# Gate and up products of both feed-forward layers: seven block products in place of eight

## What is computed

```python
def swiglu(x, w_gate, w_up, w_down):
    return (jax.nn.silu(x @ w_gate) * (x @ w_up)) @ w_down

x = layer_norm(ALPHA * x + mix.astype(x.dtype), ln_mix_g[i], ln_mix_b[i])
x = layer_norm(ALPHA * x + swiglu(x, w_ffn_gate[i], w_ffn_up[i], w_ffn_down[i]), ln_ffn_g[i], ln_ffn_b[i])
gate = jax.nn.sigmoid(x @ w_ple_gate[i] + b_ple_gate[i])
```

## Time and profile before

| | us |
|---|---|
| median of three executions | 2624.71 (2622.63 to 2624.74) |
| span of the profiled execution, first to last instruction | 2621.1 |
| median less that span | 3.6 |
| PE busy | 2516.9 (96%) |
| DVE busy | 1464.8 (56%) |
| ACT busy | 1131.0 (43%) |
| POOL busy | 149.3 (6%) |

### The profile page before, as it was taken

The page is one execution under the profiler, slowest core; times in us unless marked ns, Lnnn a source line. Parts: engine busy times, 40 slices in busy tenths (PEclk is TensorE's granted clock), DMA queues, the critical chain, the costliest instruction groups (busy, mean ns, idle before and its releaser), DMA issues.

```text
span 2621.1 us, 29230 instructions
## 1 busy us (share of the span) xinstructions
PE 2516.9 (96%) x12112; PEld 1961.0 (75%) x12112; DVE 1464.8 (56%) x1543; ACT 1131.0 (43%) x1285; POOL 149.3 (6%) x165
## 2 busy tenths in 40 slices
PE   7998996999999999999999999999989999999998
PEld 4677883888888886877757768888768667888876
DVE  3685545888888886545675343333363744323344
ACT  3423223787777776322354242222252734222223
POOL 1001011110101100000000100000100010000010
PEclk9898997999999999999999999999999999999999
DMA  7123213999999996322202222232312012232220
GB/s 272 56 99 133 101 47 154 345 363 370 359 361 358 361 358 251 154 86 83 90 2 79 97 73 83 94 105 73 113 65 101 29 55 82 77 109 97 74 95 33
DMA packets 64565, 388.74 MB, mean 148 GB/s; under 512 B 13360, under 2 KB 13488, under 8 KB 22576
## 3 DMA queue, kind: packets, MB, share of 16 engines
q1 hardware_dynamic: 53712, 373.20, 38.9%
q0 software_dynamic: 9280, 8.42, 0.9%
q10 hardware_dynamic: 1440, 5.24, 0.5%
HBM read 391.00 MB, written 20.97 MB: 157 GB/s over the span
## 4 chain that ended last, share of the span: by engine, by line
PE 87%; DVE 5%; ACT 3%; DMA 3%; issue 1%; POOL 0%; SPq 0%; ACTq 0%; DVEq 0%; POOLq 0%
PE psD L2877 72%; PE psD L2885 1%; PE psA L2050 1%; DMA ring<-w_dense 1%; DMA ring<-w_moe 1%; PE psA L1097 1%; DVE ring_r L2502 1%; PE psA L2950 1%; ACT ring_r L2286 1%; PE psA L3080 1%; PE psA L1973 1%; PE psA L3140 1%; PE psD L2100 1%; PE psA L2088 1%; PE psA L2930 1%
## 5 line engine op out<-in xcount | busy, mean ns | idle before, releaser
L2877 PE MATMUL psD<-rounded,ring_r 128*128 128x512 f32 (+1 forms) x6168 | 1456.4, 397 | 15.7 <-DVE ring_r L2502 12.3
L2877 PEld LDWEIGHTS psD<-rounded,ring_r 128*128 128x128 f32 (+1 forms) x6168 | 1155.2, 188 | 315.3 <-issue 24.0
L2502 DVE TENSOR_TENSOR ring_r<-ring,ring_r 128x2048 fp32r<-128x2048 f32 (+3 forms) x143 | 307.1, 2147 | 232.5 <-ACT ring_r L2286 228.8
L2877 PE MATMUL psD<-ring_r,rounded 128*128 128x512 f32 (+1 forms) x1728 | 412.6, 395 | 5.7 <-DVE rounded L983 2.4
L2286 ACT ACTIVATE ring_r<-ring 128x2048 fp32r<-128x2048 f32 (+3 forms) x143 | 251.9, 1762 | 366.0 <-PE psD L2877 359.5
L2877 PEld LDWEIGHTS psD<-ring_r,rounded 128*128 128x128 f32 x1728 | 320.0, 191 | 86.4 <-issue 8.7
L978 DVE TENSOR_TENSOR ring_r<-ring,ring_r 128x2048 fp32r<-128x2048 f32 x128 | 293.2, 2291 | 44.4 <-ACT ring_r L776 42.3
L776 ACT ACTIVATE ring_r<-ring 128x2048 fp32r<-128x2048 f32 x128 | 245.2, 1917 | 58.0 <-DMA ring<-w_moe 33.4
L2877 PE MATMUL psD<-rounded,rounded 128*128 128x512 f32 x768 | 192.1, 399 | 0.0
L1828 DVE TENSOR_TENSOR arena<-arena,psD 128x512 f32<-128x512 f32 x44 | 30.2, 687 | 255.3 <-ACT arena L1523 255.3
L2877 PEld LDWEIGHTS psD<-rounded,rounded 128*128 128x128 f32 x768 | 139.8, 189 | 27.6 <-issue 0.2
(11 more groups left out here) (433 smaller groups left out, 2027.5 us busy)
## 6 DMA issues: line engine op xcount, KB each, us to landing
ring<-w_moe SPq DMA_DIRECT2D x192, 1024.0 KB, 7.3
ring<-w_dense SPq DMA_DIRECT2D x134, 1024.0 KB, 4.8
ring<-w_dense SPq DMA_DIRECT2D x16, 768.0 KB, 4.1
ring<-w_dense SPq DMA_DIRECT2D x16, 640.0 KB, 3.9
arena<-x_t SPq DMA_DIRECT2D x1, 2048.0 KB, 7.9
token_rows<-arena ACTq DMA_DIRECT2D x4, 512.0 KB, 2.6
arena<-pair_rows SPq DMA_DIRECT2D x4, 512.0 KB, 7.8
arena<-pair_rows ACTq DMA_DIRECT2D x4, 512.0 KB, 8.3
```

Source lines behind the costliest of these rows:

```text
L2502: dve.tensor_tensor(lo_, ring_of(u, nk, nco), hi, ALU.subtract).then_inc(sem("w_lo"), 1)
L2877: mm = pe.matmul(out, w[a], x[b], start=start and i == 0, stop=stop_ and i == 2)
```

## The change

Of the 22 gate/up units of a layer the first two stay as they are (`PLAIN_GU = 2`). For the other 20 (numbered `s`, 0 to 19 in layer 0 and 20 to 39 in layer 1, `FAST`) the product is made from 2x2 blocks: the weights are split into gate/up and first/second half of the 1024 channels, the activations into the channel halves and the token halves (256 tokens). Eight block products become seven, with sums of blocks before and after. Each block product is 4 k-tiles x 3 matmuls of 128x256, so a unit has 84 matmuls of 256 columns (before: 48 of 512).

- **Sums of activations**, once a layer: `input_sums` makes four sums of 128x1024 on DVE, after `ln_x`; ACT and DVE split them.
- **Sums of weights**, once a unit: DVE makes the first pair S13 (one instruction, 128x1024, `first_sums`), POOL the other two, S24 (`weight_sums`, two 128x512 additions, one after the other). Both pairs are split (`pair_hi` on ACT, `pair_lo` on DVE). The unit's own cut shrinks to three quarters (128x1536).
- **Sums of products**: `first_copy` (ACT), `early_sums` (two of 256), `middle_sums`, `last_sums` (512 each) on DVE; SiLU in two pieces of 256; the product of both (`hidden`) and its split.
- **Memory**: the sums lie in raw slot 2 and their parts and the unit's parts from slot 3 on, so gate/up units and the first half's down units load into two slots instead of four (`raw_plan`). The load of the first `ple_g` unit after a feed-forward goes to slot 3 and waits until the last down unit is done. `parts_of`, `ring_of` and `loaded` follow this plan.
- Semaphores are renamed, and the constants that POOL makes for the attention wait for another signal; the work there is the same.

```diff
+                def first_sums(s):
+                    ...
+                    loaded(dve, FAST[s])
+                    dve.tensor_tensor(block_pair(S13), block_pair(raw_quarters(s, 1, 2)),
+                                      raw_quarters(s, 0).unsqueeze(1).to_broadcast([P, 2, QUARTER]), ALU.add)\
+                       .then_inc(sem("w_sums"), 1)
...
+            def weight_sums(s):
+                pool.wait_ge(sem("w_sums"), 2 * s + 1)
+                if s % N_FAST > 0:
+                    pool.wait_ge(sem("pair_lo"), 2 * s)
+                step(pool.tensor_tensor(S24[:, 0:QUARTER], S13[:, 0:QUARTER], raw_quarters(s, 2), ALU.add))
+                pool.tensor_tensor(S24[:, QUARTER:2 * QUARTER], S24[:, 0:QUARTER], raw_quarters(s, 3), ALU.add)\
+                    .then_inc(sem("w_sums"), 1)
...
+                pe.wait_ge(sem("w_lo"), SPLIT_NO[FAST[s]] + 1)
+                counted(fast(ab[:, 0, :], own, A11, tokens(0, 0), True))
+                if s == run[0]:
+                    pe.wait_ge(group_freed(before[1]), GROUP_NO[before[1]] // 2 + 1)
...
+                pe.wait_ge(sem("pair_lo"), 2 * s + 1)
+                counted(fast(dc[:, 1, :], G13, 0, sums(0), True))
+                counted(fast(dc[:, 0, :], G13, 1, sums(2), True))
+                pe.wait_ge(sem("pair_lo"), 2 * s + 2)
+                counted(fast(ab[:, 1, :], G24, 0, sums(1), True))
+                pe.wait_ge(sem("first_copy"), s + 1)
+                counted(fast(ab[:, 0, :], own, A12, tokens(4, 0), False))
+                pe.wait_ge(sem("fast_moved"), 4 * s + 2)
+                counted(fast(dc[:, 0, :], own, A22, sums(3), False))
+                fast(dc[:, 1, :], G24, 1, tokens(4, 1), False).then_inc(sem("units_done"), 1)
...
+                    if slot == 2 and done:
+                        sp_.wait_ge(sem("pair_lo"), 2 * done[-1] + 2)
+                    if slot == 3 and done:
+                        sp_.wait_ge(sem("units_done"), last_unit(("down", layer_of(done[-1]), 1, 3)) + 1)
```

The calls on DVE stand in this order (`half` 0 is the first half):

```diff
+                input_sums()
+                plain_hidden(0)
+                plain_lo(0)
+                for half, run in enumerate(halves_of(layer)):
+                    if half == 0:
+                        ahead(FAST[run[0]])
+                        first_sums(run[0])
+                        pair_lo(run[0], 0)
+                        pair_lo(run[0], 1)
+                        plain_hidden(1)
+                        plain_lo(1)
+                    for s in run:
+                        if s > run[0]:
+                            last_sums(s - 1)
+                            pair_lo(s, 1)
+                            hidden(s - 1)
+                        early_sums(s)
+                        if s < run[-1]:
+                            first_sums(s + 1)
+                        ahead(FAST[s] + 1)
+                        if s > run[0]:
+                            hidden_lo(s - 1)
+                        if s < run[-1]:
+                            pair_lo(s + 1, 0)
+                        middle_sums(s)
```

341 lines of the change are left out of this document (282 added, 59 removed).

## The result

The changed kernel takes 2637.34 us (median of six executions, 2632.55 to 2644.28), the kernel before beside it 2625.16 us (2622.63 to 2630.07): a ratio of 1.0045 [1.0029, 1.0061]. The forecast was 2635 with a range of 2612 to 2660. The profiled execution of the changed kernel has a time of 2635.92 and a span of 2634.2 us, 13.1 more than the span before.

What follows compares the result with a forecast made beforehand. PE bounds the kernel before; in the changed one DVE's queue with POOL's holds sets 10.65 us a unit. Per layer +5.2 - 2.2 + 1.4 = +4.4, two layers +8.8, with semaphores +10: 2635 us, range 2612 to 2660.

Steps and rivals of the forecast that it cites:

- 1.5 us added for semaphores: Whole kernel: allowance for the second semaphore that five of DVE's ten instructions a unit wait for, priced by no row.
- Block products on PE: Gate/up units on PE: 84 matmuls of 256 columns at 0.120 us, 10.08 us a unit against 11.20.
- rival a: Steady units: PE stays the bound at 10.08 us, POOL's additions falling beside other DVE work; total -8, 2617 us; chance 0.20.
- DVE, one unit: DVE's queue in a gate/up unit: ten instructions, 9.02 us of durations, 8.44 us with overlaps, under PE's 10.08.
- POOL against DVE: Steady units: POOL additions and two-SBUF-input DVE instructions exclude each other; each addition holds DVE 1.11 us, giving 10.66 a unit.
- PE's wait in a unit: Steady units: PE waits about half a microsecond each, except the first three of each ten, at about 10.1 us.
- Start of a layer: First gate/up half: PE waits 4 us, then until 34.4, clock loses 1.7; first unit +11.2, nine others -6.0, together +5.2.
- Second half: Second ten gate/up units: PE waits 3.6 us, 1.7 for the clock, units save 7.5; together -2.2 us a layer.
- Loads: Second half's first down unit: its load and cut end late, +1.4 us a layer; first ple unit's load hidden, 0.
- Sum: Whole kernel: +4.4 us a layer, two layers +8.8, rounded up for semaphores to +10; time 2635 us.
- b: Steady units: DVE and POOL together exceed the old 11.20, units of 11.5, +16.6 us a layer, 2658 us; chance 0.20.
- c: Starts of layers and halves: 2 to 3 us cheaper in each of four, total near 0, 2625 us; chance 0.15.

Runs made afterwards that it cites:

- no_pool: The changed kernel with GpSimd making none of the second pair's sums, only passing the semaphore on (output not the reference's): 2594.53 us.
- pool_twice: The changed kernel with one more GpSimd addition a unit, the first of the two made twice: 2681.53 us.
- one_wide: The changed kernel with one GpSimd addition of 1024 columns in place of two of 512 (output not the reference's): 2637.08 us.
- start_order: The changed kernel with the second plain unit's hidden tile ahead of the pairs' low parts and first sums ahead of the cut, at a layer's start: 2624.05 us.
- busy_starts: The changed kernel with matmuls that compute nothing put into PE's waits at the starts of a layer and of its second half: 2632.97 us.
- down_slot: The changed kernel with the second half's first down unit loaded into slot 0 instead of the slot holding the pair's sums: 2634.50 us.

## Why the prediction was right, and where its terms were off

The predicted time is 2 us from the measured one, and the mechanism is the one forecast. One term was wrong without showing in this kernel, and the layers were forecast 3 us too short each. About half of those 6 us came back through the 1.5 us added for semaphores and through a rest of the program that is 1.6 us shorter, for which the forecast has no reason: that the time is met to 2 us is in part luck.

**Block products on PE: the term that was mis-sized.** The forecast took 0.120 us for a matmul of 256 columns from 11.5 / 96 and concluded that 256 columns cost a little over half of 512. They cost half: 0.1167, 9.80 us a unit. Half of the error is the tail of 0.16 us behind the last matmul, which the busy time holds: without it the row gives 0.118. The other half is in those matmuls themselves, which ran at about the pace of no_pool's second half of layer 1 (9.89 us, 0.1178 each); why there are two paces is open. In the changed kernel it did not matter, since DVE sets the unit at 10.72. But rival a was priced by it: without the additions, with PE at its own pace, the kernel comes to about 2595 (no_pool), not 2617. Of these 22 us the 40 units at 0.28 less are 11; the rest is that a had left the starts as they are, while without the additions the waits there are 2.35 and 1.09 us instead of 4.78 and 3.56.

**DVE, one unit: right.** Forecast 8.44. The trace has 10.72 less the two holds of 1.10 and 1.09: 8.53. The 0.09 more are in the two gaps of 0.11 us ahead of instructions that need the one before, for which the forecast had 0.03.

**POOL against DVE: right, with its size.** Forecast 1.11 an addition and 10.66 a unit, if POOL gets its turn between DVE's instructions; it does, each time, and the unit is 10.72. A loop through POOL and ACT sets the unit only in pool_twice. The lock that the Trainium skill describes (SBUF — State Buffer, Who interferes with whom), where whoever is first keeps the shared port for the whole instruction, agrees with the traces, and one_wide bears it out for 1024 columns. The same page of the Trainium skill has the blocked side wait for DVE's end and some 115 ns more (A bandwidth-pool intuition that's wrong (but worth ruling out)), a figure that it took with a DMA issued from GpSimd and not with two computing engines. Those 115 ns are not seen here: an addition ends 1.16 us after DVE, less than its undisturbed 1.29, and the unit is 10.72, where the forecast's estimate by that page's figure was 11.1.

**PE's wait in a unit.** Forecast about 0.5, seen 0.65 and a few smaller gaps. Of each run of ten the forecast had three at 10.1; there is one at 9.80, then 10.58 (10.39 in the second half), then 10.72. One unit of layer 1's first half took 11.08, with DVE idle for 0.46 us between its two early sums; why is open.

**Start of a layer: right in place and size, but for the clock.** The second block product starts at 34.36 (forecast 34.4), the unit ends at 45.1 (44.8). The wait was forecast to end with the hidden tile of the second plain unit, and start_order shows that it does. The 11.2 us of the forecast less 6.0 for the other nine units is worked out with 10.65 a unit; with the 10.6 that stands beside it the term is 6.4. The clock was set at 1.7 us, after the earlier trace rows. It costs 1.9 and 2.3 by busy_starts, and 10.91 and 11.28 instead of 8.67 in the changed kernel's own rows, 2.2 and 2.6. The first half comes to +6.4, not +5.2.

**Second half: the term with the largest miss.** The wait was 3.56 (forecast 3.6). The clock cost 0.9 more, the units with only one at PE's pace some 0.9 more. Together with the load it is +1.3 where -2.2 + 1.4 = -0.8 stood.

**Loads.** Ahead of the last down products 1.74 and 1.90 (forecast 1.4), and down_slot shows that it was the load. The first ple unit's load costs nothing, as said.

**Sum.** +7.1 and +7.6 a layer where +4.4 stood. With 1.5 for semaphores the forecast had +10; the span shows +13.1. No run prices a second semaphore by itself; what the traces show in its place is the 0.09 a unit on DVE, about 3 us over the units that DVE sets.

**Rivals.** a would need POOL's additions to fall beside DVE's PSUM work; they don't, and 10.35 isn't reached. b (11.5 a unit) and c (cheap starts) didn't come: the starts cost more than forecast, not less.

## What to carry to other kernels

Work for GpSimd is not free because GpSimd is idle: if it reads SBUF while instructions with two SBUF inputs stand in the queue of a VectorE that is near the bound, each addition holds VectorE for nearly its own length (1.1 us for one of 1.29), and the same sum on VectorE itself can be cheaper (here 1.45 against 2.2 us a unit, and the kernel went from 0.45% slower to 0.9% faster). When a change shortens the bound engine, look at the first unit of every run: what stands last in the helper's queue there (a hidden tile that frees a bank, a cut that waits for a buffer) costs more than the steady state gives, and moving a few lines wins much of it back (6.6 us of 11.5 at a layer's start). Read a rate from the distance of starts in long runs, not from busy time over count, and from more than one run: two paces, 0.1167 and 0.118 us, stood side by side here.
